# Modulation vectors of a two-block transformer kernel: from streamed TensorE products to multiply-and-sum rows on VectorE

## The chip, the core and the metric

The kernel runs on one core of a Trainium2 chip: TensorE (PE, with its weight loads PEld), VectorE (DVE), ScalarE (ACT), GpSimd (POOL), SyncE (SP, here the main DMA queue) and 16 DMA engines. The metric is the device time in microseconds of one execution, lower is better.

## The reference, cut to what matters

Two transformer blocks run one after the other on 256 tokens of width 1024, all in fp32. The first block has two kinds of self-attention ("fox" and stick-breaking, "sb"), a memory cross-attention (xattn) and a mixture of 16 experts (MoE). The second has two layers over latent tokens and context tokens. Each of its layers takes six vectors of 1024 numbers, the modulation, from a condition vector; two such vectors exist, `c` for the latent and `c_ctx` for the context tokens:

```
def second_block(x, c, ctx, c_ctx, w_mod, b_mod, ...):
    for l in range(2):
        mod   = silu(c)     @ w_mod[l] + b_mod[l]      # 1024 x 6144 weights per layer
        mod_c = silu(c_ctx) @ w_mod[l] + b_mod[l]
        sh1, sc1, ga1, sh2, sc2, ga2 = split(mod, 6)   # mod_c likewise
        h = rmsnorm(x, g1[l]) * (1 + sc1) + sh1
        ...                                            # mixer: Fourier, mLSTM, latent attention
        x = x + ga1 * (mixed @ w_out[l])
        h2 = rmsnorm(x, g2[l]) * (1 + sc2) + sh2
        x = x + ga2 * (square(relu(h2 @ w_up[l])) @ w_down[l])
        # the context tokens do the same with mod_c, in layer 0 only
```

In layer 1 the context tokens need only the first two vectors of `mod_c`. The product with `w_mod` reads 48 MB of weights and needs few multiplications: it has two rows.

## The kernel before

**Weights as pieces.** All large weights are packed into one stream, `w_stream`, of pieces of 128 x 1024 numbers (512 KB). A ring of four slots holds them: SP loads a piece into `ring` (L369), ACT rounds it to `wh` (L408), DVE forms the rest `wl = ring - wh` (L1475), and PE multiplies with both (L876): each product is three matmuls, high x high, high x low and low x high. The helpers `split` and `split_turn` in the ACT and the DVE program make the next parts, three pieces ahead of PE (`AHEAD = 3`). SP refills a slot when DVE has made `wl` from it (`w_lo`), ACT overwrites a slot of `wh` when PE has begun the piece three before.

**Order of the work.** It is written out by hand, one program for each engine; engines meet only at semaphores, and every engine takes its own list in order. The stages in order of time: fox attention with the memory's keys and values (`xkv`), stick-breaking attention (`sb`, eight heads), output projection (`out1`), cross-attention (`xq`, `xat`, `xo`), router, MoE, then the two layers of the second block, each with projections, mixer, `out`, and the MLP in two halves a and b, each half an up part (16 pieces, `up`) and a down part (16 pieces, `dn`).

**The MoE loop.** Eight turns of two experts. The table `TURN` lists the pieces of a turn. An expert has six pieces: gate0, gate1, up0, up1, down0, down1. After gate1 ACT takes the SiLU; after up1 DVE multiplies (`eg`, L1755), ACT rounds to `hidh` (L617), DVE forms `hidl` (L1757), and only then can PE begin down0 (`moe_lo`). Between the expert's pieces `TURN` puts six `mod` pieces, 12 a turn and 96 in all: pieces of `w_mod`, multiplied by the stationary `cparts` (the high and low parts of both SiLU vectors). Two of them stand between up1 and down0. After every four `mod` pieces DVE transposes the result bank (L1737) and adds four small blocks into `modv` (L1740), the table of all modulation numbers.

**The MLP of layer 0.** In the up part's loop (four turns of four pieces) DVE takes in each turn, for each piece, `wl` and then `hl` (L2023, the low part of the squared activations; ACT makes the high part `hh`, L830 to L835). In the down part's loop (four turns of four pieces, two output jobs a turn) DVE takes first the four `wl` of the turn (`split_turn`), and then `down_turn`: for each of the two jobs it waits for PE (`job_full`) and adds the bank, times the gate from `modv`, to the residual `res` (L2051), which frees the bank (`job_emptied_dve`). Two banks serve the down jobs in turn: PE may begin job n only when DVE has emptied job n - 2. In half b ACT and DVE also sum squares for the next norm.

**GpSimd** does little: it loads `ctx` (L382) and the second layer's small weights (L386), and moves some rows (L394).

The lines quoted most below: L876 every matmul on ring pieces, L1475 `wl`, L408 `wh`, L2051 the residual add of the down jobs.

## Time and profile before

| what | value |
|---|---|
| three timed runs | 1900.94, 1906.58, 1911.39 us; median 1906.58 |
| profiled execution, first to last instruction | 1907.9 us |
| PE busy | 1756.0 us (92%), mean granted clock 0.944 |
| DVE busy | 1065.6 us (56%) |
| ACT busy | 917.4 us (48%) |
| POOL busy | 19.3 us (1%) |
| DMA | 242.4 MB, 127 GB/s on the mean, 264 GB/s in the MoE loop |
| MoE loop | about 383 to 759 us |
| MLP of layer 0, down parts | about 1208 to 1295 us and 1382 to 1467 us |

The profiled execution has no time printed beside its span; the span is 1.3 us above the median of the timed runs, so the two are taken as one scale. Busy shares say who works, not who sets the end: a matmul row lasts longer than the distance to the next one, since matmuls overlap, so a stage's pace on PE is read from the distances of starts.

### The profile page before, as it was taken

How to read it: one execution, taken by the hardware profiler on the slowest of the kernel's cores; microseconds unless marked ns; L12 is line 12 of the kernel's file. 1: busy time of each engine (PE TensorE's matmuls, PEld its weight loads, DVE VectorE, ACT ScalarE, POOL GpSimd, SP SyncE). 2: the span in 40 equal slices, each digit the busy share in tenths (PEclk: the TensorE clock that was granted, in tenths of full speed). 3: DMA queues.
4: the chain of work that ended last, by engine and by line, in shares of the span. 5: the costliest groups of instructions: out<-in, count | busy, mean ns of one | idle time of the engine just before them, and what ended most of it. 6: DMA issues, size and time to landing. Idle time of an engine off the chain costs nothing.

```text
span 1907.9 us, 27992 instructions
## 1 busy us (share of the span) xinstructions
PE 1756.0 (92%) x10050; PEld 1434.1 (75%) x10050; DVE 1065.6 (56%) x1646; ACT 917.4 (48%) x1397; POOL 19.3 (1%) x38
## 2 busy tenths in 40 slices
PE   6999979799999998699899989999998898989997
PEld 6976468788888887477543668888886795579997
DVE  5534364577777778692376453333334955555454
ACT  5534344456666666534456254224422454547462
POOL 0000000000000000000020000000000001000000
PEclk9999689899999999799988989999999999789999
DMA  7632022277778887123000222223222240025552
GB/s 259 203 103 89 0 89 94 95 240 261 267 269 267 269 266 270 36 91 120 15 1 1 75 69 97 96 93 96 91 99 77 89 155 0 1 97 190 173 188 90
DMA packets 68307, 242.39 MB, mean 127 GB/s; under 512 B 7312, under 2 KB 10512, under 8 KB 68112
## 3 DMA queue, kind: packets, MB, share of 16 engines
q1 hardware_dynamic: 67824, 239.71, 37.8%
q0 software_dynamic: 416, 1.77, 0.3%
q8 instruction: 45, 0.74, 0.2%
q14 instruction: 22, 0.18, 0.0%
HBM read 240.40 MB, written 1.05 MB: 127 GB/s over the span
## 4 chain that ended last, share of the span: by engine, by line
PE 72%; DVE 12%; ACT 6%; DMA 5%; issue 4%; DVEq 0%; SPq 0%; ACTq 0%
PE bank L876 71%; DMA ring<-in_w_stream 5%; DVE wl L1475 3%; ACT wh L408 2%; DVE uv L1515 1%; DVE sq L1493 1%; DVE sq L1551 1%; DVE small L1542 1%; PE bank L1034 1%; ACT sq L436 1%; DVE turned L1737 0%; ACT rstd L446 0%; ACT sq L772 0%; DVE eg L1755 0%; ACT rstd L448 0%
## 5 line engine op out<-in xcount | busy, mean ns | idle before, releaser
L1475 DVE TENSOR_TENSOR wl<-ring,wh 128x1024 fp32r<-128x1024 f32 x446 | 538.7, 1224 | 342.9 <-ACT wh L408 331.6
L876 PE MATMUL bank<-uh,wh 128*128 128x256 f32 (+3 forms) x1840 | 589.8, 321 | 43.5 <-DVE ul L1504 21.7
L408 ACT ACTIVATE wh<-ring 128x1024 fp32r<-128x1024 f32 x446 | 465.0, 1054 | 329.3 <-PE bank L876 284.9
L876 PE MATMUL bank<-ul,wh 128*128 128x256 f32 (+3 forms) x1840 | 584.7, 318 | 0.0
L876 PE MATMUL bank<-uh,wl 128*128 128x256 f32 (+3 forms) x1840 | 583.6, 317 | 0.0
L876 PEld LDWEIGHTS bank<-uh,wh 128*128 128x128 f32 (+1 forms) x1840 | 350.7, 191 | 88.4 <-issue 48.0
L876 PEld LDWEIGHTS bank<-ul,wh 128*128 128x128 f32 (+1 forms) x1840 | 351.2, 191 | 28.3
L876 PEld LDWEIGHTS bank<-uh,wl 128*128 128x128 f32 (+1 forms) x1840 | 350.7, 191 | 26.5
L876 PE MATMUL bank<-hh,wh 128*128 128x512 f32 (+1 forms) x512 | 172.7, 337 | 0.8
L876 PE MATMUL bank<-hl,wh 128*128 128x512 f32 (+1 forms) x512 | 172.1, 336 | 0.0
L876 PE MATMUL bank<-hh,wl 128*128 128x512 f32 (+1 forms) x512 | 172.1, 336 | 0.0
L2023 DVE TENSOR_TENSOR hl<-sq,hh 128x512 f32 (+1 forms) x64 | 35.8, 559 | 136.4 <-ACT hh L835 136.4
L876 PEld LDWEIGHTS bank<-hh,wh 128*128 128x128 f32 x512 | 97.2, 190 | 12.0 <-issue 2.0
L876 PEld LDWEIGHTS bank<-hl,wh 128*128 128x128 f32 x512 | 97.2, 190 | 10.0
L876 PEld LDWEIGHTS bank<-hh,wl 128*128 128x128 f32 x512 | 97.2, 190 | 9.9
L830 ACT ACTIVATE sq<-bank 128x512 f32<-128x512 f32 (+1 forms) x64 | 31.3, 489 | 113.9 <-PE bank L876 113.9
L876 PE MATMUL bank<-hidh,wh 128*128 128x256 f32 x256 | 74.9, 292 | 8.4 <-DVE hidl L1757 7.4
L876 PE MATMUL bank<-sq,table 128*128 128x256 f32 (+3 forms) x64 | 34.3, 653 | 51.2 <-DVE sq L1493 40.1
L876 PE MATMUL bank<-wh,cparts 128*68 128x512 f32 x192 | 75.5, 393 | 0.8 <-DVE modv L1740 0.8
L876 PE MATMUL bank<-wl,cparts 128*68 128x512 f32 x192 | 75.5, 393 | 0.0
L876 PE MATMUL bank<-hidh,wl 128*128 128x256 f32 x256 | 72.4, 283 | 0.0
L876 PE MATMUL bank<-hidl,wh 128*128 128x256 f32 x256 | 72.4, 283 | 0.0
(240 smaller groups left out, 2041.1 us busy)
## 6 DMA issues: line engine op xcount, KB each, us to landing
ring<-in_w_stream SPq DMA_DIRECT2D x446, 512.0 KB, 3.9
table<-in_table SPq DMA_DIRECT2D x1, 1849.5 KB, 12.5
res<-in_x SPq DMA_DIRECT2D x4, 256.0 KB, 3.8
res<-in_mem SPq DMA_DIRECT2D x1, 1024.0 KB, 14.7
res<-in_ctx POOLq DMA_DIRECT2D x1, 1024.0 KB, 6.2
out_dram<-res SPq DMA_DIRECT2D x1, 1024.0 KB, 4.8
lw<-in_small SPq DMA_DIRECT2D x1, 704.0 KB, 15.7
lw<-in_small POOLq DMA_DIRECT2D x1, 704.0 KB, 4.3
```

What stands on the lines that cost most here:

```text
L408: act.activation(wh[:, s, :], ring[:, s, :], ACT.Copy).then_inc(S("w_hi"), 1)
L436: act.activation(dst, src, ACT.Square).then_inc(S("norm_sq"), 1)
L830: act.activation(r, bank[(b0 + j) % 4][:, 0:n], ACT.Relu).then_inc(S("job_emptied_act"), 1)
L876: ins = pe.matmul(*operands, **flags)
L1034: last = pe.transpose(bank[6][:, to * P:(to + 1) * P], prob[i % 2][:, j * P:(j + 1) * P], ident)
L1475: tt(wl[:, s, :], ring[:, s, :], wh[:, s, :].bitcast(F32), ALU.subtract).then_inc(S("w_lo"), 1)
L1493: tt(sq[0:p, 3, 0:n], sq[0:p, 3, 0:n], sq[0:p, t % 2, 0:n], ALU.add).then_inc(S("norm_add"), 1)
L1515: last = stt(o, src, g, r, ALU.mult, ALU.mult)
L1542: dve.tensor_reduce(smv(i, 0, 0, g), b, AX_X, ALU.max, negate=True).then_inc(S("sm_max"), 1)
L1551: last = ts(p, p, smv(i, 1, k), None, ALU.mult)
L2023: tt(hl[:, d, 0:n].rearrange("p a b -> p (a b)"), sq[:, 2 + j % 2, 0:n], hh[:, d, 0:n].rearrange("p a b -> p (a b)").bitcast(F32), ALU.sub ...
```

## The change

The 96 `mod` pieces leave the stream and `TURN`: a turn now has 12 pieces in place of 24, and down0 stands right behind up1. In their place the transposed `w_mod` lies in a new DRAM tensor as 96 tiles of 128 output columns x 1024 (512 KB each), and both SiLU vectors are computed as rows, written to DRAM (`c_rows`) and loaded back as a copy on every partition (`mod_c`). A tile and a vector make one row instruction: `tensor_tensor_reduce` multiplies the two, 1024 numbers a partition, and sums them into one column of `modv`; it is the kernel's `dot` (result thrown away into `spent_to`) or `mod_last` (result thrown away into the tile itself). A tile of layer 0 takes two such rows, one for `c` and one for `c_ctx`; of layer 1, 16 tiles take two and 32 take one. The rows number 160.

Layer 0's 48 tiles are spread as follows: one behind each of the eight sb heads, 2 in `out1`, 3 in `xq`, 3 in `xo`, and 4 a turn in the MoE loop, one behind each down piece's `wl`. Layer 1's 48 tiles stand in the MLP of layer 0, three in each of its 16 loop turns (`late_mods`). POOL loads the tiles through two slots (`mod_loads`): it issues a tile's load when DVE has used the tile that lay in the slot before (`mod_used`). In `late_mods` tiles one and three of a turn share slot 0, and DVE takes all three in one go. Where they stand in a turn: at its start in the up loop, between the four `wl` and `down_turn` in the down loop. The bias and the gains of layer 1 (`mod_bias(1)`) are applied behind the MLP of layer 0 in place of ahead of layer 0, and layer 1's small weights are loaded by POOL behind the last tile.

```diff
-N_MOE = 12 * NE
+N_MOE = 6 * NE
...
-TURN = []
-for _e in range(2):
-    for _what in ("gate0", "mod", "gate1", "mod", "up0", "mod", "up1", "mod", "mod", "down0", "mod", "down1"):
-        if _what == "mod":
-            _n = [w for w, _, _ in TURN].count("mod")
-            TURN.append(("mod", _n // 4, _n % 4))
-        else:
-            TURN.append((_what[:-1], _e, int(_what[-1])))
+TURN = [(_what, _e, _m) for _e in range(2) for _what in ("gate", "up", "down") for _m in range(2)]
 N_TURN = len(TURN)
-MOD_STEPS = (8, 19, 23)
+MOD_SB, MOD_OUT, MOD_XQ, MOD_XO, MOD_TURN = 1, 2, 3, 3, 4
+MOD_MOE = 8 * MOD_SB + MOD_OUT + MOD_XQ + MOD_XO
+N_MOD = 48
+assert MOD_MOE + 8 * MOD_TURN == N_MOD
+MOD_ORDER = [(0, t) for t in range(N_MOD)]
+for _r in range(16):
+    MOD_ORDER += [(1, _r), (1, 16 + 2 * _r), (1, 17 + 2 * _r)]
+MOD_SLOT = [g % 2 for g in range(N_MOD)] + [0, 1, 0] * 16
...
+        uh_f32 = at("uh_f32", [P, KT, 2 * T], uh_at)
+        late_slot = [at("mod_w0", [P, 1024], lw_at), at("mod_w1", [P, 1024], sq_at + 2048)]
+        late_c = at("mod_c", [P, 2, 1024], rows_at + 512)
+        mod_w = [[uh_f32[:, 4 * k:4 * k + 4, CTX] for k in range(2)], [late_slot[k][:, :] for k in range(2)]]
+        mod_c = [[uv[:, 4 * k:4 * k + 4, CTX] for k in range(2)], [late_c[:, k, :] for k in range(2)]]
...
-            for l in range(1, NL):
-                pool.wait_ge(S("job_full"), JOBS.full(JOBS.number(f"va_{l - 1}", 3)))
-                pool.dma_start(lw[:, :], small_in[l]).then_inc(S(f"lw_in{l}"), 16)
+            pool.wait_ge(S("c_silu"), 1)
+            pool.dma_start(c_rows, c_work[:, 0, :]).then_inc(S("c_out"), 16)
+            pool.wait_ge(S("c_out"), 16)
+            def mod_loads(l):
+                c_all = c_rows.rearrange("(o r) k -> o (r k)", o=1)
+                for k in range(2):
+                    src = c_all[:, k * 1024:(k + 1) * 1024].to_broadcast([P, 1024])
+                    if l == 0:
+                        src = src.rearrange("p (a b) -> p a b", a=4)
+                    pool.dma_start(mod_c[l][k], src).then_inc(S("mod_c_in"), 16)
+                for g in range(l * N_MOD, (l + 1) * N_MOD):
+                    before = [f for f in range(l * N_MOD, g) if MOD_SLOT[f] == MOD_SLOT[g]]
+                    if before:
+                        pool.wait_ge(S("mod_used"), before[-1] + 1)
+                    src = mod_stream[g]
+                    if l == 0:
+                        src = src.rearrange("p (a b) -> p a b", a=4)
+                    pool.dma_start(mod_w[l][MOD_SLOT[g]], src).then_inc(S(f"mod_in{MOD_SLOT[g]}"), 16)
+            pool.wait_ge(S("job_full"), JOBS.full(JOBS.number("xkv", 7)))
+            mod_loads(0)
...
+                if l + 1 < NL:
+                    pool.wait_ge(S("job_full"), JOBS.full(JOBS.number(f"out_{l}", 0)))
+                    mod_loads(l + 1)
+                    pool.wait_ge(S("mod_used"), (l + 2) * N_MOD)
+                    pool.dma_start(lw[:, :], small_in[l + 1]).then_inc(S(f"lw_in{l + 1}"), 16)
...
-                    elif what == "mod":
-                        q, b = e, bank[6 + e % 2]
-                        if m == 0:
-                            pe.wait_ge(S("mod_in"), i * 3 + (2 if q == 2 else 1))
-                        parts_turn(i, N_TURN, n)
-                        for k in range(2):
-                            c = cparts[:, 4 * (2 * m + k):4 * (2 * m + k) + 68]
-                            mm(b[0:68, :], c, wh[:, n % RING, k * 512:(k + 1) * 512], start=(m + k == 0), stop=False)
-                            last = mm(b[0:68, :], c, wl[:, n % RING, k * 512:(k + 1) * 512], start=False,
-                                      stop=(m == 3 and k == 1))
-                        if m == 3:
-                            last.then_inc(S("mod_full"), 1)
...
+            mod_at = [0]
+            def dot(l, k, which, out, spent_to):
+                dve.tensor_tensor_reduce(out=spent_to, in0=mod_w[l][k], in1=mod_c[l][which], scale=1.0, scalar=0.0,
+                                         op0=ALU.mult, op1=ALU.add, accum_out=out)
+            def mod_last(l, k, which, out):
+                return dve.tensor_tensor_reduce(out=mod_w[l][k], in0=mod_w[l][k], in1=mod_c[l][which], scale=1.0,
+                                                scalar=0.0, op0=ALU.mult, op1=ALU.add, accum_out=out)
+            def mod_tiles(n, spent_to):
+                for _ in range(n):
+                    g = mod_at[0]
+                    if g == 0:
+                        dve.wait_ge(S("mod_c_in"), 32)
+                    k = MOD_SLOT[g]
+                    dve.wait_ge(S(f"mod_in{k}"), 16 * (g // 2 + 1))
+                    if g:
+                        dve.wait_ge(S("mod_used"), g)
+                    dot(0, k, 1, modv[:, 2 * g + 1:2 * g + 2], spent_to)
+                    mod_last(0, k, 0, modv[:, 2 * g:2 * g + 1]).then_inc(S("mod_used"), 1)
+                    mod_at[0] += 1
...
+                if h < NF:
+                    mod_tiles(MOD_SB, pair[0][:, :].rearrange("p (a b) -> p a b", a=4))
...
+            def add_to_res(phase, name, first, mods):
                 for s in range(4):
                     split(first + 2 * s + 1 + AHEAD - (s == 3))
+                    if s < mods:
+                        mod_tiles(1, spent[:, :, :])
...
-                def modulation(q):
-                    dve.wait_ge(S("mod_full"), i * 3 + (q + 1))
-                    ch.link(dve.transpose(turned[:, :, :].rearrange("p a b -> p (a b)"), bank[6 + q % 2][0:32, :]))
-                    for c in range(4):
-                        o = modv[32 * c:32 * c + 32, bass.ds(i * 24 + 8 * q, 8)].rearrange("p (t w) -> p t w", w=2)
-                        last = tt(o, turned[:, c:16:4, 0:2], turned[:, c:16:4, 2:4], ALU.add)
-                    last.then_inc(S("mod_in"), 1)
-                    dve.wait_ge(S("mod_in"), i * 3 + (q + 2))
+                ch.loop(i, 2 + 1)
+                def mod_turn(t):
+                    g = MOD_MOE + t
+                    k = MOD_SLOT[g]
+                    dve.wait_ge(S(f"mod_in{k}"), i * (16 * MOD_TURN // 2) + 16 * (g // 2 + 1))
+                    dve.wait_ge(S("mod_used"), i * MOD_TURN + g)
+                    dot(0, k, 1, macc[:, 2 * t + 1:2 * t + 2], spent[:, :, :])
+                    ins = mod_last(0, k, 0, macc[:, 2 * t:2 * t + 1])
+                    ins.then_inc(S("mod_used"), 1)
+                    return ins
...
+                    if what == "down":
+                        mod_turn(2 * e + m)
+                dve.wait_ge(S("mod_used"), i * MOD_TURN + (MOD_MOE + MOD_TURN))
+                ch.link(dve.tensor_copy(modv[:, bass.ds(i * (2 * MOD_TURN) + 2 * MOD_MOE, 2 * MOD_TURN)], macc[:, :]))
...
+                    def late_mods(r0, i):
+                        r = N_MOD + 3 * r0
+                        if r0 == 0:
+                            dve.wait_ge(S("mod_c_in"), 64)
+                        spent_to = pair[2][:, :]
+                        dve.wait_ge(S("mod_in0"), i * 32 + (16 * (N_MOD // 2) + 32 * r0 + 16))
+                        dot(1, 0, 1, macc[:, 1:2], spent_to)
+                        mod_last(1, 0, 0, macc[:, 0:1]).then_inc(S("mod_used"), 1)
+                        dve.wait_ge(S("mod_in1"), i * 16 + (16 * (N_MOD // 2) + 16 * r0 + 16))
+                        mod_last(1, 1, 0, macc[:, 2:3]).then_inc(S("mod_used"), 1)
+                        dve.wait_ge(S("mod_in0"), i * 32 + (16 * (N_MOD // 2) + 32 * r0 + 32))
+                        mod_last(1, 0, 0, macc[:, 3:4]).then_inc(S("mod_used"), 1)
+                        dve.wait_ge(S("mod_used"), i * 3 + (r + 3))
+                        dve.tensor_copy(modv[:, bass.ds(i * 2 + (2 * N_MOD + 2 * r0), 2)], macc[:, 0:2])
+                        last = dve.tensor_copy(modv[:, bass.ds(i * 4 + (2 * N_MOD + 32 + 4 * r0), 4)]
+                                               .rearrange("p (a b) -> p a b", b=2)[:, :, 0:1],
+                                               macc[:, 2:4].rearrange("p (a b) -> p a b", b=1))
+                        last.then_inc(S("macc_out"), 1)
+                        dve.wait_ge(S("macc_out"), i + (r0 + 1))
                     with dve.Fori(0, MC // 4) as i:
+                        if l == 0:
+                            late_mods(8 * half, i)
...
                         split_turn(i, 4, pd, AHEAD, AHEAD + 3)
+                        if l == 0:
+                            late_mods(8 * half + 4, i)
                         down_turn(i)
```

On PE, between an expert's up1 and down0 in the MoE loop (L876 and L916 are the same helper in the two kernels; `cparts` marks a `mod` piece, `hidh` and `hidl` the first matmuls of down0), the kernel before has:

```order
L876 MATMUL bank<-uh,wl 128x256
L897 REGISTER_ALU
L876 MATMUL bank<-wh,cparts 68x512 [waits w_lo]
L876 MATMUL bank<-wl,cparts 68x512
...
L1194 REGISTER_ALU
L897 REGISTER_ALU [waits moe_lo]
L876 MATMUL bank<-hidh,wh 128x256 [waits w_lo]
L876 MATMUL bank<-hidl,wh 128x256
```

and the changed kernel:

```order
L916 MATMUL pair<-ul,wh 128x256
L916 MATMUL pair<-uh,wl 128x256
L1222 REGISTER_ALU
L937 REGISTER_ALU [waits moe_lo]
L916 MATMUL pair<-hidh,wh 128x256 [waits w_lo]
L916 MATMUL pair<-hidl,wh 128x256
```

The eight `cparts` matmuls that stood between the last matmul of up1 and the wait for `moe_lo` are gone.

On DVE, in the down loop of layer 0's MLP, from the last `wl` of a turn to the first residual add, the kernel before has:

```order
L1474 REGISTER_ALU
L1475 TENSOR_TENSOR wl<-ring,wh 128x1024 [waits w_hi]
L2038 ISA
L2051 ISA [waits job_full]
L2051 SCALAR_TENSOR_TENSOR res<-bank,modv,res 128x256
L2051 ISA
L2051 SCALAR_TENSOR_TENSOR res<-bank,modv,res 128x256
```

and the changed kernel (the ISA rows of L1611 and L1616 with two inputs are the row instructions, those with none write out the sum):

```order
L1503 TENSOR_TENSOR wl<-ring,wh 128x1024 [waits w_hi]
L1611 ISA pair,macc<-mod_w_100,mod_c 128x1024 [waits mod_in0]
L1616 ISA mod_w_100,macc<-mod_w_100,mod_c 128x1024
L1616 ISA mod_w_101,macc<-mod_w_101,mod_c 128x1024 [waits mod_in1]
L1616 ISA mod_w_100,macc<-mod_w_100,mod_c 128x1024 [waits mod_in0]
...
L2095 ISA [waits mod_used]
L2095 COPY modv<-macc 128x2
L2124 REGISTER_ALU [waits macc_out]
L2137 ISA [waits job_full]
L2137 SCALAR_TENSOR_TENSOR res<-pair,modv,res 128x256
```

The three tiles of `late_mods`, with their waits for both slots and for `mod_used`, now stand between the last `wl` and the wait for `job_full`.

## Rows read from the trace of the kernel before

**Rows 1.** The page: busy time of each engine, and the chain that ended last.
```profile
PE 1756.0 (92%) x10050; PEld 1434.1 (75%) x10050; DVE 1065.6 (56%) x1646; ACT 917.4 (48%) x1397; POOL 19.3 (1%) x38
PE 72%; DVE 12%; ACT 6%; DMA 5%; issue 4%; DVEq 0%; SPq 0%; ACTq 0%
```
**Rows 2.** Busy by stage: us, each engine busy (count), clock, DMA share, GB/s.
```profile
186.00:245.00 59.00, 50.23 (x141) 26.22 (x138) 21.32 (x36) 21.52 (x37) 0.00 (x0) 0.71 0.00 0
383.50:758.70 375.20, 365.93 (x2665) 325.80 (x2663) 290.01 (x371) 234.15 (x239) 0.00 (x0) 1.00 0.79 264
```
**Rows 3.** Timeline, one expert in the MoE loop: start, us, engine, instruction.
```profile
509.75 0.39 PE L876 MATMUL bank<-wh,cparts 128*68 128x512 f32 x1
510.68 0.28 PE L876 MATMUL bank<-uh,wh 128*128 128x256 f32 x1
513.52 0.39 PE L876 MATMUL bank<-wh,cparts 128*68 128x512 f32 x1
513.72 0.69 DVE L1755 TENSOR_TENSOR eg<-bank,eg 128x512 f32<-128x512 f32 x1
514.44 0.63 ACT L617 ACTIVATE hidh<-eg 128x512 fp32r<-128x512 f32 x1 [2.25 <-DVE eg L1755]
515.11 0.69 DVE L1757 TENSOR_TENSOR hidl<-eg,hidh 128x512 fp32r<-128x512 f32 x1 [0.70 <-ACT hidh L617]
515.93 0.38 PE L876 MATMUL bank<-hidh,wh 128*128 128x256 f32 x1 [0.41 <-DVE hidl L1757]
```
**Rows 4.** Waits of PE in the MoE loop: us in total, times, longest.
```profile
PE bank L876 <- DVE hidl L1757: 7.4, 16, 0.7
```
**Rows 5.** Groups by line: count, busy, mean ns of one, idle before.
```profile
L1475 DVE TENSOR_TENSOR wl<-ring,wh 128x1024 fp32r<-128x1024 f32 x446 | 538.7, 1224 | 342.9 <-ACT wh L408 331.6 <-DVE sq L2033 0.4
L1616 DVE SCALAR_TENSOR_TENSOR sbt<-table,sbt 128x512 f32<-128x512 f32 x8 | 5.5, 692 | 0.3
L478 ACT ACTIVATION_READ_ACCUMULATOR sq<-bank,small 128x1 f32 x48 | 9.4, 195 | 0.0
```
**Rows 6.** Timeline, a turn of layer 0's down loop.
```profile
1220.21 1.23 DVE L1475 TENSOR_TENSOR wl<-ring,wh 128x1024 fp32r<-128x1024 f32 x1 [4.21 <-ACT wh L408]
1221.36 0.87 DVE L2051 SCALAR_TENSOR_TENSOR res<-bank,modv,res 128x256 f32 x2
1224.13 0.39 PE L876 MATMUL bank<-hh,wh 128*128 128x512 f32 x1
```
**Rows 7.** DMA issues (down loop's window, then the page): count, KB, us to landing.
```profile
ring<-in_w_stream SPq DMA_DIRECT2D x15, 512.0 KB, 3.4
lw<-in_small POOLq DMA_DIRECT2D x1, 704.0 KB, 4.3
```
**Rows 8.** Busy by stretch, around pauses of PE; columns as in rows 2.
```profile
351.17:353.35 2.18, 0.00 (x2) 0.00 (x1) 1.98 (x3) 1.42 (x2) 0.00 (x0) 0.98 0.37 150
353.35:355.42 2.07, 2.07 (x4) 1.17 (x4) 1.23 (x1) 0.16 (x1) 0.00 (x0) 0.50 0.00 0
906.04:908.09 2.05, 0.00 (x1) 0.03 (x1) 0.63 (x1) 1.84 (x3) 0.00 (x0) 1.00 0.00 0
908.09:911.50 3.41, 3.41 (x8) 1.35 (x9) 1.54 (x3) 1.87 (x3) 0.00 (x0) 1.00 0.00 0
1106.41:1111.23 4.82, 0.00 (x1) 0.03 (x1) 3.40 (x9) 3.81 (x8) 0.00 (x0) 0.50 0.37 109
1111.23:1114.43 3.20, 3.20 (x8) 2.52 (x9) 3.20 (x9) 1.82 (x5) 0.00 (x0) 0.50 0.00 0
1114.43:1117.43 3.00, 3.00 (x15) 2.42 (x14) 3.00 (x9) 1.68 (x4) 0.00 (x0) 1.00 0.02 5
```
**Rows 9.** Timeline, DVE in the sb stage, heads 1 and 7.
```profile
190.22 0.69 DVE L1611 SCALAR_TENSOR_TENSOR sbt<-bank,sbt 128x512 f32<-128x512 f32 x1 [0.39 <-ACT sbt L547]
238.53 0.69 DVE L1611 SCALAR_TENSOR_TENSOR sbt<-bank,sbt 128x512 f32<-128x512 f32 x1 [2.34 <-ACT sbt L547]
```
**Rows 10.** Timeline, start of layer 0's up loop in half a.
```profile
1120.52 1.21 DVE L1475 TENSOR_TENSOR wl<-ring,wh 128x1024 fp32r<-128x1024 f32 x1
1128.43 0.60 ACT L830 ACTIVATE sq<-bank 128x512 f32<-128x512 f32 x1 [8.33 <-PE bank L876]
```

More of the change, by code:

```diff
@@ L1653, in add_to_res @@
                 split(first + 7 + AHEAD)
-            add_to_res("out1", "xattn", S_OUT)
+            add_to_res("out1", "xattn", S_OUT, MOD_OUT)
             norm_tiles("xattn", res, "g_xattn", LAT, LAT)
-            split(S_XQ + 7 + AHEAD)
+            for s in range(4):
+                split(S_XQ + 2 * s + 1 + AHEAD)
+                if s < MOD_XQ:
+                    mod_tiles(1, spent[:, :, :])
             a = UNIT0["xat"]
@@ L1773, in _, with mod_bias @@
             add_square("fin1", 3, P, 512)
[L1774 to L1775 removed]
+            def mod_bias(l):
+                m = modv[:, 2 * N_MOD * l:2 * N_MOD * (l + 1)]
+                ch.link(tt(m, m, tab("b_mod")[:, 2 * N_MOD * l:2 * N_MOD * (l + 1)], ALU.add))
                 for k2 in range(2):
@@ L2110, in pack @@
     slots += placed([(0, f["w_router_group"][0]), (4, f["w_router_expert"][0])])
-    mods = [s for l in range(NL) for s in moving(f["w_mod_2"][l], 0, 6 * D, 2, 512)]
-    mods = iter(mods)
     for turn in range(NE // 2):
         for what, e, m in TURN:
-            if what == "mod":
-                slots.append(next(mods))
-            elif what == "down":
+            if what == "down":
                 slots.append(f["w_exp_down"][0, 2 * turn + e][m * P:(m + 1) * P, :])
```

58 lines of the change are left out of this document (29 added, 29 removed).

## The prediction

> **What bounds the kernel now.** I read the busy times and the chain first, then the busy table by stage, then the timeline of the stages that the change touches. PE is busy 92% of the span and carries 72% of the chain [rows 1], so what leaves PE in a stage that PE bounds is gained, and what holds PE up there is lost. The MoE loop is such a stage: PE is busy 365.9 of 375.2 us at full clock, DVE 290, ACT 234 [rows 2]. The reader should not take its 0.79 DMA share and 264 GB/s for the bound: PE would then wait for `wl`, and in the loop's list of waits the main one is for `hidl`, 7.4 us in 16 waits [rows 4]. The sb stage runs at a mean clock of 0.71 with DVE busy a third of the time [rows 2]. In the down loops of layer 0 PE runs without a pause, and DVE has slack, but it takes its list in order, so what counts there is where its slack lies.
>
> **MoE loop, what goes.** One `mod` piece takes PE from 509.75 to 510.68, 0.93 us; an ordinary piece from 510.68 to 513.52, 2.84 us [rows 3]. 96 x 0.93 = 89 us leave PE.
>
> **MoE loop, what comes.** After up1 PE needs `hidl`: DVE begins `eg` at 513.72, ACT follows at 514.44, DVE again at 515.11, and PE's first down0 matmul starts at 515.93 [rows 3]. The last matmul of up1 gives way at 513.52, so the chain takes 2.41 us. Before, two `mod` pieces covered all but 0.46 us of it (7.4 / 16, [rows 4]); now nothing stands there. That is 1.95 us more for each of 16 experts, 31 us. Net: 89 - 31 = 58 us gained.
>
> **The row instruction.** No trace shows it. The nearest row is `wl`, also two SBUF inputs of 128 x 1024 fp32: 1.224 us alone, and 1.15 us from one start to the next instruction's (1220.21 to 1221.36) [rows 5, 6]. Writing out the sum is a second instruction; ACT's like one takes 0.195 us [rows 5]. I take 1.3 us a row, so 2.6 us a tile with two rows; the lower end is 1.15 (readout hidden), the upper 2.5 (twice the 1.15 of `wl`, plus 0.2 of readout). I take the low side because `wl` is the same shape.
>
> The Trainium skill, "Vector Engine (DVE) Microarchitecture Reference", section "7. Points that are easy to get wrong", says that the scalar-tensor-tensor form with two SBUF sources that aren't bf16 halves throughput, as no port is left for the accumulator. The trace has that form without an accumulator at 692 ns for 512 columns [rows 5], which is the full rate; with one it has none. By the page a row would take 2.5 us; this is the second rival below.
>
> **DVE and DMA in the MoE loop.** An expert now gives DVE six `wl` (about 7), the expert's own small operations (about 2) and two tiles (5.2), 14 us, against PE's 6 x 2.84 + 2.41 = 19.4. The tiles stand behind down0's and down1's `wl`, where DVE has two pieces of lead, and it has caught up by the next gate1. Transfers: an expert needs eight times 512 KB in 19.4 us, 216 GB/s, where 264 already flow [rows 2]. Both hidden; without that cover the second rival applies. The 96 `wl` and 96 `wh` that go gave nothing that PE waited for.
>
> **Clock in the MoE loop.** PE's pause of 2.4 us an expert can lower the granted clock. The trace has both cases: behind a pause of 2.18 us the clock was 0.50 (1.2 GHz), behind one of 2.05 us it stayed at 1.00 (2.4 GHz) [rows 8]. A stretch at half clock behind the pause costs half its length; I take 3.2 us, as in the one full stretch shown (1111.23 to 1114.43), in about six of the 16 experts: 6 x 1.6 = 10 us. Bounds: 0, and 16 x 3.2 = 51 if every pause costs twice that.
>
> **Down loops of layer 0, the main cost.** Each turn's three tiles stand between DVE's fourth `wl` and the residual adds. Today DVE ends that `wl` at 1221.36 and empties the turn's first bank by 1222.2 (two adds, 0.87 us); PE comes to the next turn's first job, which needs that bank, at 1224.13 [rows 6]. The slack is 1.8 us with the semaphore. Now the block's length D comes before the add. Two rows on tile one: 2.6. Then POOL may load tile three into the same slot, while DVE takes tile two (1.3, hidden): 512 KB land in 3.4 us from SP's queue, 704 KB in 4.3 from POOL's [rows 7]; I take 3.6 with 0.2 for waking POOL. Tile three: 1.3. Two small copies, three waits and register work: about 1.0. D = 2.6 + 0.2 + 3.6 + 1.3 + 1.0 = 8.7 us. PE stands still for 8.7 - 1.8 = 6.9 us in each of eight turns, 55 us. By D's ends: 1.15 us rows, 3.4 us transfer and 0.5 us for the rest give 2.3 + 3.4 + 1.15 + 0.5 = 7.35, a stall of 5.5, 44 us; 2.5 us rows and 4.3 us transfer give 5.0 + 4.5 + 2.5 + 1.0 = 13, 11.2 a turn, 90 us. Behind the stalled DVE stand the other job's add and the next turn's `wl`; these do PE no further harm, since PE stood still as well.
>
> The Trainium skill, "DMA: Bandwidth & Descriptors", section "Anatomy of one DMA — SWDGE (gpsimd) path", fits 2.0 us plus bytes over 436 GB/s, 3.2 us here, 3 us less over the eight turns than my 3.6 gives.
>
> **Clock in the down loops.** A pause of 4.82 us lowered the clock, which stayed at half for 3.2 us after PE resumed [rows 8]. Seven stalls (the eighth runs into a norm, where PE pauses anyway) should each leave 3 to 6 us at half clock, at a cost of 2.2 each: 15 us. Bounds 0 and 21. Down loops together: 55 + 15 = 70 us.
>
> **Up loops.** The same block stands at a turn's start. PE then has three pieces of some 5.4 us ready (4.21 idle and 1.23 busy between two `wl`, [rows 6]), 16 us; DVE comes to the block behind the last job's ACT and DVE work, by my estimate 3 us into the turn, and 3 + 8.7 + 1.2 = 13 us: hidden, with 3 us to spare, so a block of up to 12 us stays free. Only the first turn of half a is not: DVE gets there at 1120.5, needs 8.7 + 1.2 and has the fourth `wl` at 1130.4, while ACT's first job result at 1128.43 marks PE's end with the first three pieces [rows 10]. 2 us.
>
> **The rest.** In the sb stage DVE waits 2.34 us a head for ACT at full clock and more at half clock [rows 9], so a 2.6 us tile costs 0.3 us in three or four heads; head 0 has only 0.39 us before head 1's row [rows 9], but PE reaches the operation that needs it some 5 us later. The first tile's loads start at the end of `xkv`, ten us ahead. In `out1`, `xq` and `xo` a tile fits the wait for the job's second piece. The last tile of the MoE loop delays the residual by 1 us. Together 3 us, at most 8. The SiLU rows, the split bias and POOL's late load of `lw` I cost at nothing: the first lie under `wl` work, the last has 100 us until it is used.
>
> **Sum.** -58 + 10 + 70 + 2 + 3 = +27 us. The profiled span of 1907.9 becomes 1935; the median of the timed runs lies 1.3 us lower, so 1934 us.
>
> **Rivals.** *The clock holds* (other side). The point: whether pauses of 2.4 and 6.9 us are short enough not to lower it. For it: the 2.05 us pause at 906 us [rows 8]. Against it: 2.18 and 4.82 did. Then -58 + 55 + 2 + 3 = +2, or 1909 us; with D at its lower end too, 44 in place of 55, 1898: no longer slower. *Rows at half rate.* Against it: `wl`'s row. Then the down loops cost 90 + 15, DVE needs 19 us an expert and bounds the MoE loop with PE (I put 2 us an expert, 32), sb heads lose 2 us each (16): -58 + 10 + 32 + 105 + 16 + 5 = +110, 2017 us. *Every MoE pause halves the clock for long.* 51 in place of 10: 1975 us. *The MoE gain is not there, since transfers were the bound*: PE's busy share says no; it would give 1934 + 58, 1992 us.
>
> **How the numbers follow.** Forecast with its own range 1915 to 1955: 0.60. Clock holds or short block: 0.22, of which about half ends below 1897. Half rate 0.08, bad MoE clock or bound by transfers 0.10. The range 1899 to 1980 leaves out about a tenth on either side. A change of 0.5% (9.5 us, 1897 to 1916) is about what can be told from none: faster 0.12, same 0.16, slower 0.72.
>
> **What would show it.** In the changed profile: PE waits 16 times for `hidl`, 2.3 us each; the MoE loop takes 320 to 330 us; row instructions near 1.2 us; in each down turn of layer 0 PE waits 6 to 8 us for the residual add, with clock 0.5 behind it; DVE in `late_mods` waits 2 to 3 us for tile three's DMA. The forecast is wrong if that wait is absent, if the rows take over 2 us, or if `dn` turns keep their 21.8 us.

## The result, and the profile after

The changed kernel takes 1943.34 us (median of 4 runs, 1937.98 to 1946.2) against 1903.76 us for the kernel before on the same chip: ratio 1.0205, 95% interval 1.0173 to 1.0237. That is 2% slower, between 1.7 and 2.4%. The profiled execution has a span of 1941.7 us and was itself timed at 1943.49, so a time is its span and 1.8 us. The mean granted clock fell from 0.944 to 0.921.

The page's busy times of the changed kernel, and the chain that ended last by engine:

```profile
PE 1706.3 (88%) x9670; PEld 1412.2 (73%) x9670; DVE 1111.2 (57%) x1788; ACT 822.5 (42%) x1301; POOL 84.2 (4%) x139
PE 77%; DVE 11%; ACT 5%; issue 4%; DMA 2%; DVEq 0%; SPq 0%; ACTq 0%
```

PE is busy 50 us less than before, and yet the kernel is longer: the busy shares, set beside [rows 1], hide what the change did.

The two stretches that matter, first in the kernel before (columns as in [rows 2]): the loop over experts with its lead-in, up to its last product, and the MLP of layer 0.

```profile
370.36:758.68 388.32, 379.02 (x2756) 338.38 (x2756) 291.00 (x373) 241.25 (x249) 0.00 (x0) 1.00 0.77 256
1111.23:1466.24 355.01, 355.01 (x1536) 289.52 (x1536) 126.69 (x159) 128.77 (x178) 0.00 (x0) 1.00 0.28 95
```

The same two in the changed kernel, then stretches around single pauses of PE:

```profile
375.28:713.31 338.03, 302.04 (x2376) 298.36 (x2376) 222.19 (x293) 146.32 (x153) 22.53 (x30) 0.95 0.59 194
1072.39:1490.66 418.27, 372.18 (x1536) 299.88 (x1536) 201.58 (x312) 128.14 (x177) 24.03 (x46) 0.94 0.40 137
418.40:420.65 2.25, 0.01 (x1) 0.00 (x1) 1.39 (x2) 0.63 (x1) 0.00 (x0) 1.00 0.58 197
420.65:423.50 2.85, 2.85 (x24) 2.85 (x24) 1.33 (x2) 1.06 (x1) 0.00 (x0) 1.00 0.15 56
438.18:440.42 2.24, 0.00 (x0) 0.00 (x1) 1.38 (x2) 0.63 (x1) 0.00 (x0) 0.94 0.64 194
440.42:443.58 3.16, 3.16 (x15) 3.16 (x16) 1.45 (x2) 1.06 (x1) 0.00 (x0) 0.50 0.10 41
1248.36:1254.84 6.48, 0.00 (x0) 0.00 (x0) 3.13 (x9) 0.00 (x0) 1.31 (x3) 0.82 0.34 97
1254.84:1259.37 4.53, 4.52 (x11) 3.56 (x12) 1.88 (x3) 1.06 (x1) 0.00 (x0) 0.50 0.67 232
```

The loop over experts is 388.3 - 338.0 = 50.3 us shorter; the MLP of layer 0 is 418.3 - 355.0 = 63.3 us longer, and the wait for the next norm, behind that stretch, takes 8.8 us in place of 2.8. Read the pauses in pairs: a pause, and the stretch of work behind it. Behind the 2.25 us pause at 418 the clock stays at 1.00, and 24 matmuls take 2.85 us; behind the equal one at 438 it is 0.50, and 15 matmuls take 3.16. So it goes on through the loop: 1.2 GHz (a granted clock of 0.50) behind every second of the 16 pauses, eight in all, and 2.4 GHz behind the others. Behind each of the seven long waits in the MLP the clock is 0.50, and so it is behind the norm's wait that takes the place of an eighth.

The waits of the changed kernel: engine, line, what it waited for, us in total, times, longest.

```profile
PE pair L916 <- DVE res L2137: 46.3, 8, 7.2
PE pair L916 <- DVE sq L2143: 10.3, 2, 8.8
PE pair L916 <- DVE hidl L1816: 36.0, 16, 2.2
DVE mod_w L1616 <- DMA mod_w<-in_mods: 47.1, 16, 3.6
```

The wait for `hidl` answers to [rows 4]: 36.0 us in place of 7.4. The one for `res` was not there before; seven of its eight lie in the MLP of layer 0 and last 6.4 to 7.2 us, 46.1 us together. The stall of the last turn shows as the longer wait for `sq`, the squares of the next norm.

Where PE leaves up1 for down0 (answers to [rows 3]), timeline of the changed kernel:

```profile
437.89 0.28 PE L916 MATMUL pair<-uh,wl 128*128 128x256 f32 x1
438.22 0.69 DVE L1814 TENSOR_TENSOR eg<-pair,eg 128x512 f32<-128x512 f32 x1 [0.44 <-PE pair L916]
438.94 0.63 ACT L657 ACTIVATE hidh<-eg 128x512 fp32r<-128x512 f32 x1 [2.42 <-DVE eg L1814]
439.60 0.69 DVE L1816 TENSOR_TENSOR hidl<-eg,hidh 128x512 fp32r<-128x512 f32 x1 [0.69 <-ACT hidh L657]
440.42 0.58 PE L916 MATMUL pair<-hidh,wh 128*128 128x256 f32 x1 [2.25 <-DVE hidl L1816]
```

One turn of the down loop, on the right of the fourth `wl` (answers to [rows 6]):

```profile
1244.28 1.23 DVE L1503 TENSOR_TENSOR wl<-ring,wh 128x1024 fp32r<-128x1024 f32 x1 [4.22 <-ACT wh L448]
...
1245.42 1.23 DVE L1611 CUSTOM_DVE_ANT_0 pair<-mod_w,mod_c 128x1024 f32<-128x1024 f32 x1
...
1246.56 0.14 DVE L1611 DVE_READ_ACCUMULATOR2_ANT macc<- 128x1 f32 x1
1246.56 1.22 DVE L1616 CUSTOM_DVE_ANT_0 mod_w<-mod_w,mod_c 128x1024 f32<-128x1024 f32 x1
...
1247.71 1.22 DVE L1616 CUSTOM_DVE_ANT_0 mod_w<-mod_w,mod_c 128x1024 f32<-128x1024 f32 x1
...
1248.09 0.53 POOL L415 DMA_DIRECT2D mod_w<-in_mods  x1 [24.24 <-DVE macc L1616]
...
1251.85 1.23 DVE L1616 CUSTOM_DVE_ANT_0 mod_w<-mod_w,mod_c 128x1024 f32<-128x1024 f32 x1 [2.92 <-DMA mod_w<-in_mods]
...
1253.83 1.66 DVE L2137 SCALAR_TENSOR_TENSOR res<-pair,modv,res 128x256 f32 x4 [0.27 <-DVE modv L2096]
1254.85 0.79 PE L916 MATMUL pair<-hh,wh 128*128 128x512 f32 x1 [6.49 <-DVE res L2137]
```

The block of three tiles lasts from 1245.42 to 1253.83, 8.4 us. Its longest piece is not a row instruction but a load: the load of tile three can start only when tile one's slot is free (1248.09), and its data are used 3.76 us later (1251.85). The page's line on these loads, the medians from issue to landing (answers to [rows 7]):

```profile
mod_w<-in_mods POOLq DMA_DIRECT2D x48, 512.0 KB, 3.8
```

`down_turn`'s adds stand behind all that, and PE behind the adds.

The row instructions of the changed kernel by form, and their readouts (answers to [rows 5]):

```profile
L1616 DVE CUSTOM_DVE_ANT_1 uh_f<-uh_f,uv 128x1024 f32<-128x1024 f32 x48 | 58.6, 1221 | 0.0
L1611 DVE CUSTOM_DVE_ANT_0 pair<-mod_w,mod_c 128x1024 f32<-128x1024 f32 x16 | 19.6, 1227 | 1.7 <-DMA mod_w<-in_mods 1.7
L1611 DVE DVE_READ_ACCUMULATOR2_ANT macc<- 128x1 f32 x48 | 4.9, 103 | 0.0
```

A row instruction costs what a `wl` costs: 1.22 us, 1.15 from start to start (1246.56 to 1247.71, above). Its readout, the second instruction, which writes out the sum, starts at the same time as the next row instruction (both 1246.56) and so adds nothing there.

### The profile page after: what moved, and what is told of

It is laid out like the page before. It is cut to its first block, busy times and chain, and to the rows that moved or that the text cites. A ratio compares the mean times of both kernels' runs of the same rounds, so it can differ in the third digit from the quotient of the medians.

```text
span 1941.7 us, 26692 instructions
## 1 busy us (share of the span) xinstructions
PE 1706.3 (88%) x9670; PEld 1412.2 (73%) x9670; DVE 1111.2 (57%) x1788; ACT 822.5 (42%) x1301; POOL 84.2 (4%) x139
## 4 chain that ended last, share of the span: by engine, by line
PE 77%; DVE 11%; ACT 5%; issue 4%; DMA 2%; DVEq 0%; SPq 0%; ACTq 0%
PE pair L916 77%; DMA mod_w<-in_mods 2%; ACT wh L448 1%; DVE wl L1503 1%; DVE uv L1543 1%; DVE pair L1611 1%; PE pair L1074 1%; DVE sq L1521 1%; DVE hidl L1816 1%; DVE eg L1814 1%; DVE sq L1579 1%; DVE small L1570 1%; ACT hidh L657 1%; ACT sq L476 0%; ACT sq L812 0%
## 5 line engine op out<-in xcount | busy, mean ns | idle before, releaser
L916 PE MATMUL pair<-uh,wh 128*128 128x256 f32 (+3 forms) x1840 | 591.2, 321 | 49.5 <-DVE ul L1532 21.8
L1503 DVE TENSOR_TENSOR wl<-ring,wh 128x1024 fp32r<-128x1024 f32 x350 | 426.2, 1224 | 362.6 <-ACT wh L448 352.7
L916 PE MATMUL pair<-ul,wh 128*128 128x256 f32 (+3 forms) x1840 | 589.3, 320 | 0.0
L916 PE MATMUL pair<-uh,wl 128*128 128x256 f32 (+3 forms) x1840 | 586.9, 319 | 0.0
L916 PEld LDWEIGHTS pair<-uh,wh 128*128 128x128 f32 (+1 forms) x1840 | 353.5, 192 | 90.4 <-issue 53.1
L916 PEld LDWEIGHTS pair<-ul,wh 128*128 128x128 f32 (+1 forms) x1840 | 351.5, 191 | 26.6
L916 PEld LDWEIGHTS pair<-uh,wl 128*128 128x128 f32 (+1 forms) x1840 | 351.1, 191 | 26.6
L916 PE MATMUL pair<-hh,wh 128*128 128x512 f32 (+1 forms) x512 | 178.7, 349 | 40.3 <-DVE res L2137 39.5
L916 PE MATMUL pair<-hl,wh 128*128 128x512 f32 (+1 forms) x512 | 176.4, 345 | 0.0
L916 PE MATMUL pair<-hh,wl 128*128 128x512 f32 (+1 forms) x512 | 176.2, 344 | 0.0
L916 PEld LDWEIGHTS pair<-hh,wh 128*128 128x128 f32 x512 | 100.3, 196 | 54.9 <-issue 44.0
L916 PE MATMUL pair<-hidh,wh 128*128 128x256 f32 x256 | 79.7, 311 | 36.0 <-DVE hidl L1816 36.0
L916 PEld LDWEIGHTS pair<-hl,wh 128*128 128x128 f32 x512 | 100.3, 196 | 10.8
L916 PEld LDWEIGHTS pair<-hh,wl 128*128 128x128 f32 x512 | 99.8, 195 | 11.2
L916 PE MATMUL pair<-sq,table 128*128 128x256 f32 (+3 forms) x64 | 34.9, 661 | 58.6 <-DVE sq L1521 42.3
L1616 DVE CUSTOM_DVE_ANT_0 mod_w<-mod_w,mod_c 128x1024 f32<-128x1024 f32 x48 | 57.5, 1223 | 47.1 <-DMA mod_w<-in_mods 47.1
L916 PEld LDWEIGHTS pair<-hidh,wh 128*128 128x128 f32 x256 | 54.4, 212 | 39.2 <-issue 39.2
L916 PE MATMUL pair<-hidl,wh 128*128 128x256 f32 x256 | 77.5, 303 | 0.0
L916 PE MATMUL pair<-hidh,wl 128*128 128x256 f32 x256 | 76.8, 300 | 0.0
```

Source lines behind the costliest of these rows:

```text
L916: ins = pe.matmul(*operands, **flags)
L1503: tt(wl[:, s, :], ring[:, s, :], wh[:, s, :].bitcast(F32), ALU.subtract).then_inc(S("w_lo"), 1)
L1616: return dve.tensor_tensor_reduce(out=mod_w[l][k], in0=mod_w[l][k], in1=mod_c[l][which], scale=1.0, scalar=0.0, op0=ALU.mult, op1=ALU.add, ...
```

## The experiments

Each starts from the changed kernel; "a gain" is against its 1943.3 us. The kernel before ran beside all of them, at 1903 to 1904 us as in the first comparison, so the times can be set side by side.

**The down loops: where the three tiles stand.** First the tiles behind the adds:

```diff
                         split_turn(i, 4, pd, AHEAD, AHEAD + 3)
+                        down_turn(i)
                         if l == 0:
                             late_mods(8 * half + 4, i)
-                        down_turn(i)
```

> In the four turns of each down loop of layer 0 the three late tiles stand behind the adds to the residual instead of ahead of them; nothing else changes. Theory (VectorE serves in order, and the adds that empty TensorE's two banks stand behind 8.4 us of tiles): the eight TensorE waits of 6.4 to 7.2 us fall back to the 1.5 us or so that the up loops show, or less, and the half-clock stretch behind each goes. 8 x 6.6 = 53 us of waits and 8 x 2.2 = 17 us of half clock, less 2 us that may come back through the next turn's weight splits: 1943 - 68 = 1875 us (1867 to 1888). Rival (the work of the tiles itself, on VectorE or in the DMA queues, costs the time wherever it stands): 1943 +- 6 us. Rival (the splits of the next turn's weights, now behind the tiles, become the late thing): TensorE waits on split weights in the down loops by 3 to 5 us a turn, 1900 to 1915 us.

Measured: 1885.75 us (1883.81 to 1888.65), a gain of 57.6. The waits for `res` are gone, so the rival on the tiles' own work falls; but 10 us of the forecast gain are missing. Its waits on PE, and the MLP of layer 0:

```profile
PE pair L916 <- DVE ul L1534: 22.6, 4, 10.2
PE pair L916 <- DVE wl L1503: 9.7, 4, 6.2
1068.10:1432.89 364.79, 358.62 (x1536) 291.76 (x1536) 197.99 (x309) 128.62 (x178) 23.68 (x45) 0.98 0.45 157
```

The third mechanism of the expectation did come, but at a seam, not in each turn: where half a's last block of tiles meets the block of half b's first up turn, two blocks stand in a row, and PE waits 6.2 us for a split weight, with half clock behind the wait. The longest wait for `ul` is 10.2 us in place of 4.9: layer 1's first norm stands behind the last block.

Second, only the third tile behind the adds:

```diff
                         if l == 0:
-                            late_mods(8 * half + 4, i)
+                            late_mods(8 * half + 4, i, 0)     # tiles one and two alone
                         down_turn(i)
+                        if l == 0:
+                            late_mods(8 * half + 4, i, 1)     # tile three and the two copies
```

> In the down loops of layer 0 the first two late tiles stay ahead of the adds; the third, with the two copies of the sums, goes behind them. Theory (the length of what stands ahead of the adds sets the stall, and more than half of it is the third tile's wait for its own load, which can only start when the first tile is used): 3.7 us stand ahead instead of 8.4, so a stall goes from 6.6 to 1.9 us, 8 x 4.7 = 38 us back, and some of the half-clock stretches with them (8 x 0 to 2.2): 1943 - 38 - 9 = 1896 us (1886 to 1908). Rival (any late tile ahead of the adds costs a wait of the same kind, because the first wait for a load is the long one): no more than 10 us back, 1933 to 1943 us.

Measured: 1885.43 us (1883.11 to 1890.16), a gain of 57.9 where 47 were expected. Its wait for the adds, and the MLP of layer 0:

```profile
PE pair L916 <- DVE res L2148: 10.9, 8, 1.6
1067.43:1436.26 368.83, 357.49 (x1536) 288.59 (x1536) 200.32 (x312) 127.97 (x177) 23.93 (x46) 1.00 0.45 155
```

The stall follows the length of what stands ahead of the adds: seven waits of 1.5 to 1.6 us (three row instructions, 3.45 us, less the slack of 1.9) in place of 6.5. None of these seven lowered the clock (mean 1.00 over the stretch), so what PE's work took longer at half clock came back whole: PE is busy 357.5 us in the stretch in place of 372.2, 14.7 us less, where 9 were expected.

Third, no late tiles at all. This kernel leaves out layer 1's products with `w_mod`, so it is no version to use, only a price:

```diff
-                    mod_loads(l + 1)
-                    pool.wait_ge(S("mod_used"), (l + 2) * N_MOD)
...
-                            late_mods(8 * half, i)
...
-                            late_mods(8 * half + 4, i)
```

> The late tiles and their loads are left out: layer 1's modulation vectors are the bias alone. Everything of layer 0 stays. This gives the whole price of layer 1's 48 tiles, wherever it is paid. Theory: 8 stalls (53 us), their half clock (17 us), and 1 us at the two up loops' starts: 1943 - 71 = 1872 us (1865 to 1880), within 6 us of the run in which they stand behind the adds. Rival (the 24 MB of their loads slow the weight stream in the up loops too, or the rows there delay the splits): the up loops of layer 0 get shorter by over 5 us as well, 1865 us or less, well below the run with the tiles behind the adds.

Measured: 1865.55 us (1864.74 to 1866.4), a gain of 77.8, and 20.2 below the first of these three. The spans of the two differ by 18.0 us: 364.79 - 356.24 = 8.6 in the MLP of layer 0, the first seam with its half clock; 5.4 in the wait for layer 1's norm, the second; the other 4 in layer 1 itself, where the half-clock stretches fall otherwise. MLP of layer 0:

```profile
1068.88:1425.12 356.24, 356.24 (x1536) 290.24 (x1536) 126.66 (x159) 128.61 (x178) 0.00 (x0) 0.99 0.29 94
```

Last, the tiles at the head of the turn:

```diff
-                        split_turn(i, 4, pd, AHEAD, AHEAD + 3)
                         if l == 0:
                             late_mods(8 * half + 4, i)
+                        split_turn(i, 4, pd, AHEAD, AHEAD + 3)
                         down_turn(i)
```

> In the down loops of layer 0 the three late tiles stand at the head of the turn, ahead of the four weight splits of that turn (and so four splits ahead of the adds, some 20 us of TensorE's work). The run with the tiles behind the adds left 20 us against the run without them; its trace puts them at two seams: a 6.2 us wait for a split weight where the last down turn's tiles meet the first up turn's, and 5.4 us more where layer 1's first norm waits for the last block. Theory (a block of 8.4 us is free wherever a split's three pieces of lead, 15 us, stand between it and what TensorE waits for): no wait in the loops and none at either seam, the time of the run without late tiles plus 2 to 4 us: 1869 us (1864 to 1876). Rival (a block of 8.4 us ahead of a split is late in its turn, and TensorE waits for the first split of each down turn): 8 x 3 to 6 us, 1890 to 1915 us.

Measured: 1872.09 us (1867.48 to 1874.51), a gain of 71.3. MLP of layer 0:

```profile
1069.38:1425.17 355.79, 355.19 (x1536) 289.18 (x1536) 203.12 (x319) 128.62 (x178) 24.74 (x47) 1.00 0.47 164
```

355.8 us with all 48 tiles, 355.0 without them in the kernel before: in this stretch the same work costs 63 us or 0.8, by its place in DVE's list. The whole kernel is not as clean: by the medians it takes 6.5 us more than the one without late tiles, while the two spans differ by 1.1 us, since this trace is of the fastest of five executions. Where the other 5 us lie is not shown.

**The clock by itself.** TensorE is kept at work inside the waits by products that nobody reads:

```diff
                             last.then_inc(S("job_full"), 1)
+                        if l == 0:
+                            for f in range(26):
+                                mm(bank[6][:, 0:n], wh[:, (pd + 3) % RING, 0:P], hh[:, 15, 0:n], start=True, stop=True)
```

> Late tiles stay ahead of the adds. At the end of each down turn of layer 0 TensorE runs 26 more products of 512 columns (some 5.6 us, into a bank that nothing reads) inside the time in which it would wait. Theory (the granted clock falls because TensorE stands still): the waits shrink to about 1 us, the adds come at the same time as before, and the half-clock stretch of 6.8 us behind each of the eight stalls, 4.4 us of it under work, is gone: 8 x 2.2 = 17 us back, 1926 us (1919 to 1933). Rival (the clock falls on its own there, or the stall itself is the whole cost): 1943 us (1939 to 1949).

Measured: 1923.89 us (1916.23 to 1926.75), a gain of 19.5. Two rows of its timeline at a turn's end, and a stretch with four turns:

```profile
1238.52 6.05 PE L916 MATMUL pair<-hh,wh 128*128 128x512 f32 x26
1245.08 0.49 PE L916 MATMUL pair<-hh,wh 128*128 128x512 f32 x1 [0.50 <-DVE res L2140]
1160.00:1290.00 130.00, 127.79 (x558) 104.21 (x558) 56.69 (x88) 25.08 (x28) 7.88 (x15) 1.00 0.40 132
1067.49:1476.72 409.23, 405.35 (x1744) 328.75 (x1744) 203.97 (x319) 127.95 (x177) 24.73 (x47) 0.99 0.42 141
```

The adds free the bank no sooner: from the first idle product to the first that counts it takes 6.6 us (1238.52 to 1245.08), as long as the pause it fills, 6.5. Yet the clock stays at 1.00. So the half clock is the pause's doing, and a part of the loss of its own. Its size is read best in the place: the MLP and the wait behind it take 409.2 + 2.9 us in place of 418.3 + 8.8, so 14.9 us come back. (The last turn's idle products lie inside the stretch, hence the short wait.) The span of this trace, of the fastest of five executions, is 27 us shorter; the other 12 us lie ahead of the MLP and behind it, where the edit changes nothing and the half-clock stretches fall otherwise. The same in the loop over experts:

```diff
                         if m == 0:
+                            for f in range(19):
+                                mm(bank[6][:, 0:T], uh[:, 0, T:T + P], uh[:, 0, LAT], start=True, stop=True)
                             pe.wait_ge(S("moe_lo"), i * 2 + (e + 2))
```

> Ahead of TensorE's wait for the hidden activations of each expert stand 19 more products of 256 columns (some 2.1 us, into a bank that nothing reads). Theory (the wait itself lets the granted clock fall behind every second expert): the 16 waits shrink from 2.25 to about 0.1 us, the eight half-clock stretches of 3.4 us in the loop go, 3.2 us of each under work: 8 x 1.6 = 13 us back, 1930 us (1925 to 1937). Rival (the clock follows something else than the wait): 1943 us, up to 1948 where the extra products overhang.

Measured: 1932.55 us (1925.52 to 1936.21), a gain of 10.8; the loop is shorter by just that, at clock 0.99 in place of 0.95:

```profile
371.86:699.11 327.25, 327.23 (x2680) 323.84 (x2680) 221.47 (x293) 146.30 (x153) 22.53 (x30) 0.99 0.59 200
```

**The loop over experts: do the rows cost anything there?**

```diff
-                    dot(0, k, 1, macc[:, 2 * t + 1:2 * t + 2], spent[:, :, :])
-                    ins = mod_last(0, k, 0, macc[:, 2 * t:2 * t + 1])
+                    ins = dve.memset(macc[:, 2 * t:2 * t + 2], 0.0)
```

> In the mixture-of-experts loop the 32 tiles are loaded as before, but their 64 rows are not computed (a tiny clear of two columns stands where the pair of rows stood, so layer 0's later modulation vectors are wrong). Theory (the rows lie beside the down products, ahead of nothing that TensorE waits for; the 2.25 us wait for the hidden activations is the chain from the last up product through VectorE and ScalarE): no change, 1943 us (1938 to 1948), with the 16 waits still 2.25 us each. Rival (the rows delay the weight splits or the gate's activation, and the 16 waits or the stretches between them grow by it): 16 x 1 to 2.4 us, 1905 to 1930 us.

Measured: 1937.58 us (1935.12 to 1940.12), ratio to the kernel before 1.0184 (1.0162 to 1.0206), which overlaps that of the changed kernel: by the times alone the 5.8 us are not settled. (Without its rows this kernel leaves out part of layer 0's modulation.) The loop, and the pause behind it:

```profile
369.09:709.87 340.78, 304.79 (x2376) 301.12 (x2376) 153.87 (x202) 146.18 (x153) 22.53 (x30) 0.95 0.56 193
709.87:714.77 4.90, 0.01 (x2) 0.00 (x1) 4.53 (x8) 2.46 (x4) 0.00 (x0) 0.77 0.34 107
```

With 68 us of DVE work less the loop is no shorter (340.8 against 338.0, the clock falling behind nine pauses instead of eight). Behind it PE waits 4.9 us for the norm instead of 7.7: the last tiles' rows stood ahead of the adds there. That is 2.8 us; its span is 7.6 us shorter, but 6.2 of them lie ahead of the loop, where it is the same as the changed kernel.

**The gain that the loop can give.** The pieces are turned by one, so that the next expert's gate0 stands where the `mod` pieces stood (with one gate piece ahead of the loop, one idle piece at its end, and gate0 waiting for the SiLU of the expert before):

```diff
-TURN = [(_what, _e, _m) for _e in range(2) for _what in ("gate", "up", "down") for _m in range(2)]
+TURN = [("gate", 0, 1), ("up", 0, 0), ("up", 0, 1), ("gate", 1, 0), ("down", 0, 0), ("down", 0, 1),
+        ("gate", 1, 1), ("up", 1, 0), ("up", 1, 1), ("gate", 2, 0), ("down", 1, 0), ("down", 1, 1)]
```

> The order of the pieces in the loop over experts is turned by one: the first gate piece of the next expert stands between the last up piece and the first down piece of this one (one gate piece ahead of the loop, one idle piece of zeros at its end), so that the wait for the hidden activations is covered as it was before the change. Theory: a gate piece lasts 2.7 us, the chain 2.25 to 2.4 us, so 16 waits of 2.25 = 36 us go, with the eight half-clock stretches behind them, 13 us, against 2.9 us for the idle piece: 1943 - 46 = 1897 us (1890 to 1903). Rival (something behind the hidden activations is late too, such as the weight splits on VectorE, whose turn holds the rows): waits on split weights take the place of those, and no more than half comes back, 1918 to 1943 us.

Measured: 1893.17 us (1890.59 to 1896.5), a gain of 50.2, which by itself brings the change below the kernel before (ratio 0.9948, 0.9932 to 0.9965), as the moved tiles did by themselves (0.9908 for the first two placements, 0.9828 at the head). PE is busy all the way; the stretch holds the 96 pieces of the experts and the idle one:

```profile
371.99:661.74 289.75, 289.75 (x2400) 289.55 (x2400) 222.70 (x294) 145.62 (x154) 22.53 (x30) 0.99 0.68 228
```

**Together.** This order of pieces with the first down-loop edit:

> Both edits together: the next expert's gate piece ahead of this expert's down pieces, and the late tiles behind the adds in layer 0's down loops. Theory (the two losses are separate): 1943 - 68 - 46 = 1829 us (1818 to 1842), about 4% below the kernel before the change, whose streamed products and their 96 pieces are what is then saved. Rival (both losses hide one limit, such as the weight stream or VectorE's queue): 1860 us or more.

Measured: 1834.2 us (1832.62 to 1836.25), a gain of 109.1, against 57.6 + 50.2 = 107.8 for the two apart. With the tiles at the head of the turn instead:

> The tiles at the head of the down turns together with the next expert's gate piece ahead of this expert's down pieces. The second edit gave 50 us by itself and 51 us beside the tiles behind the adds; if the two stay separate: 1869 - 50 = 1819 us (1812 to 1828). Rival (some 10 us of the first edit were the clock's chance): 1830 us or more.

Measured: 1825.33 us (1818.96 to 1830.36), a gain of 118.0, against 71.3 + 50.2 = 121.5. And with the last two places where a tile stood ahead of an add:

```diff
-                    if s < mods:                     # in add_to_res: from ahead of the add
-                        mod_tiles(1, spent[:, :, :])
                     b = full(dve, phase, s)
...
+                    if s < mods:                     # ... to behind the add and the square
+                        mod_tiles(1, spent[:, :, :])
...
-                    if what == "down":
-                        mod_turn(2 * e + m)
+                    if step in (0, 4, 5, 10):
+                        mod_turn((0, 4, 5, 10).index(step))
```

> The kernel before this, and two smaller moves: in the xattn and ffn sums the tile stands behind the add and its square instead of ahead of the add, and in the loop over experts the last tile of a turn goes to the turn's first step, so that no rows stand between the last down products and the adds behind the loop. Theory (what is left of the change's cost in front of and behind the loop is VectorE's order there): the wait ahead of the ffn norm falls from 4.0 to the 2.2 us of the kernel before, the one behind the loop from 7.7 to 4.9 us, and 0 to 4 us of half clock go with them: 4.6 + 2 = 6 us below the kernel before this, 1813 us (1806 to 1819). Rival (those two waits end on something else): no change, 1819 us.

Measured: 1817.59 us (1809.36 to 1819.41), ratio to the kernel before 0.9537 (0.9514 to 0.956). Its busy times, the pause ahead of the ffn norm, 2.18 us as in [rows 8], and the one behind the loop over experts, 5.2 us in place of 7.7:

```profile
PE 1663.1 (92%) x9694; PEld 1386.5 (77%) x9694; DVE 1109.5 (61%) x1789; ACT 823.5 (46%) x1302; POOL 83.8 (5%) x139
351.25:353.43 2.18, 0.01 (x1) 0.01 (x1) 1.98 (x3) 1.43 (x2) 0.00 (x0) 1.00 0.85 329
658.65:663.83 5.18, 0.01 (x1) 0.01 (x1) 4.77 (x10) 2.46 (x4) 0.00 (x0) 0.89 0.33 107
```

It is the best version, 4.6% below the kernel before, where the change as it was placed had made a loss of 2%. Not all of this belongs to the change: the turned order of the pieces was not tried on the kernel before, where it could give back at most PE's idle time in the loop, 388.3 - 379.0 = 9.3 us.

## Why the prediction was right

Forecast 1934 us, measured 1943.3. The spans moved by 33.8 us, against +27 in the sum: -50.3 in the loop over experts, +69.6 in the MLP of layer 0 with the waits behind it, +14.4 in the rest. So the two large terms held, 20 us apart and of opposite sign, and the small ones did not. The rest of the 9 us is the step from span to time: I took 1.3 us off the span, but a time is the span and 1.8 us. The median moved by 39.6 us, more than the spans, since the profiled execution of the kernel before was a long one: at 1907.9 + 1.8 us it lies 5.9 above this comparison's median.

- **Loop over experts, -48 forecast, -50.3 measured.** The chain came as forecast: from start to start it takes 2.41 us (up1's last matmul begins at 437.89 and gives way 0.12 later, down0 begins at 440.42). But 2.25 us of it are idle, since a matmul row lasts longer than the distance to the next one, and the 0.46 us that I took off were such an idle part. Like from like, the waits grew by 36.0 - 7.4 = 28.6 us, not 31. The clock fell behind eight pauses, not six, for 3.2 us of work each (440.42 to 443.58 above): 12.6 us against 10; the kept-busy run gave 10.8 back. The two errors cancel, and that is luck: nothing in the kernel before said six. -89 + 28.6 + 12.6 = -47.8. Of the 2.5 us left, 1.9 are idle time of PE in the old loop outside that wait (388.32 - 379.02 - 7.4), of which the new loop has none (338.03 - 302.04 - 36.0); the sum had no term for it.
- **Rows and their cover there.** The run without rows has an equally long loop. Right.
- **The row instruction, 1.3 us taken.** 1.15 us from start to start. The Trainium skill ("Vector Engine (DVE) Microarchitecture Reference", section "7. Points that are easy to get wrong") says of the scalar-tensor-tensor form that two SBUF sources that aren't bf16 halve its throughput. The row instruction, which the trace shows under another name, is not slowed so: 1.22 us for 1024 columns of fp32 is `wl`'s own time [rows 5]. Whether it has the form that the page means, no run here shows. With it falls the rival at 2017 us.
- **Down loops, +70 forecast, +69.6 measured** (63.3 in the stretch, 6.3 from its end to layer 1's first product). D was 8.4 us, not 8.7. The seven stalls inside the stretch sum to 46.1 us, the eighth adds 6: 52 against 55. The clock fell behind each of the seven, with 3.9 to 4.6 us of half clock under work, 15 us in all as forecast; the kept-busy run gave 14.9 back. About 2 us more of half clock lie at the stretch's start: PE is busy 372.2 - 355.0 = 17.2 us longer. Tile three's load took 3.76 us from issue to its first row, against 3.6.
- **Up loops, +2 forecast.** PE waited for no split weight there in the changed kernel's trace. In the run with the blocks at the head of all 16 turns the wait that I forecast in half a's first turn is 0.6 us, and the whole MLP of layer 0 is 0.8 us longer than before: less than forecast.
- **The rest, +3 forecast, +14.4 by the two traces.** This term was too small, but by how much one trace of each cannot say. Two parts are DVE's order: the pause ahead of the ffn norm takes 4.0 us against 2.18 [rows 8], where I had put the tile down as fitting the wait for the job's second piece, and the norm behind the loop waits 7.7 us instead of 6.6. The last kernel took both back by moving the tiles (2.18 and 5.2). The others are 3.1 us more ahead of the loop over experts, 5.4 in the mixer and 3.0 in layer 1, and there the clock moves the time by itself: from PE's first product to the loop the changed kernel takes 365.6 us and the seven experiments that are the same up to there take 359.5 to 366.6, with 56 to 72 us of it at half clock, against 359.9 in the kernel before. In layer 1 the runs that compute it whole lie between 427.8 and 437.5 us, against 435.2 here and 432.2 before. I have no experiment that sets these parts apart from the clock.
- **Rivals.** "The clock holds" is refuted by the trace and by both kept-busy runs. "Transfers are the bound" falls with the turned order: the loop over experts ran at 228 GB/s and PE never stood still.

## What to carry to other kernels

On an engine that serves in order, price new work by what stands behind it and by the slack there, and not by the engine's busy share: with three tiles a turn ahead of the adds the MLP of layer 0 took 63 us longer, with the same tiles four weight splits earlier 0.8 us. Only what the block lasts beyond the slack is paid, and a wait for a load inside the block counts as part of it. When work is taken off the bounding engine, ask which of its pieces covered another engine's chain, and put something else there.
